# A transformer layer on one core: the product p @ w_ple computed beside the mixer's last blocks, not beside the last gate

## What is computed

```python
for i in range(DEPTH):                                  # DEPTH = 1
    proj = rms_norm(h, norm_mix[i]) @ w_in[i]           # q, k, v of two attention mixers A and B
    oa = sliding_window_sink_attention(...)             # 8 heads, window of 128
    ob = differential_attention(...)                    # 4 heads, 8 query blocks of 128 each
    h = h + jnp.concatenate([oa, ob], axis=-1) @ w_out[i]
    h = h + gated_conv_ffn(rms_norm(h, norm_ffn[i]), ...)
    gate = jax.nn.sigmoid(rms_norm(h, norm_ple[i]) @ w_ple_gate[i])
    h = h + gate * (p[i] @ w_ple[i])                    # p: 1024 x 256, w_ple: 256 x 1024
return rms_norm(h, norm_final)
```

## Time and profile before

| | before |
|---|---|
| median of 3 runs (range) | 1261.01 us (1259.12 to 1261.21) |
| the profiled execution, its own time | 1262.01 us |
| its span in the trace | 1259.9 us |
| TensorE busy | 1219.5 us (97%) |
| VectorE busy | 868.3 us (69%) |
| ScalarE busy | 517.3 us (41%) |
| mean granted TensorE clock | 0.99 |

### The profile page before, as it was taken

The page is one execution under the profiler, slowest core; times in us unless marked ns, Lnnn a source line. Parts: engine busy times, 40 slices in busy tenths (PEclk is TensorE's granted clock), DMA queues, the critical chain, the costliest instruction groups (busy, mean ns, idle before and its releaser), DMA issues.

```text
span 1259.9 us, 17110 instructions
## 1 busy us (share of the span) xinstructions
PE 1219.5 (97%) x6167; PEld 1004.0 (80%) x6167; DVE 868.3 (69%) x1510; ACT 517.3 (41%) x1042; POOL 248.5 (20%) x291
## 2 busy tenths in 40 slices
PE   8999999999789999999999999999999999999997
PEld 7997787887667787888888888888888888888885
DVE  5423786777886466887787777877677898964442
ACT  4311664665664224433333333333344444643321
POOL 0000000354454122232323323223120000000000
PEclk9999999999899999999999999999999999999998
DMA  7464233112833411333332323223398533620101
GB/s 210 91 89 87 51 85 84 31 43 72 219 124 61 141 50 59 101 110 99 112 98 85 125 88 122 84 84 125 135 326 317 174 94 104 222 67 25 43 34 50
DMA packets 128668, 136.07 MB, mean 108 GB/s; under 512 B 15570, under 2 KB 93130, under 8 KB 128522
## 3 DMA queue, kind: packets, MB, share of 16 engines
q1 hardware_dynamic: 128586, 135.00, 35.6%
HBM read 96.77 MB, written 37.22 MB: 106 GB/s over the span
## 4 chain that ended last, share of the span: by engine, by line
PE 63%; issue 2%; DVE 2%; DMA 1%; SPq 0%; ACT 0%; POOL 0%; POOLq 0%; DVEq 0%
PE ps L1687 62%; PE ps L1693 1%; DMA act_t<-mix_a 1%; DVE xs L1453 0%; PE ps L1927 0%; DVE h L1448 0%; DVE conv L1392 0%; SPq L479 0%; POOL stat L678 0%; ACT xs L787 0%; DVE act_t L1167 0%; PE ps L2077 0%; DVE gel L1680 0%; DVE h L1669 0%; DVE conv L1666 0%
## 5 line engine op out<-in xcount | busy, mean ns | idle before, releaser
L1687 PE MATMUL ps<-act_t,wbuf 128*128 128x512 f32 x1200 | 290.0, 398 | 2.9 <-DVE wbuf L1167 2.9
L1687 PEld LDWEIGHTS ps<-act_t,wbuf 128*128 128x128 f32 x1200 | 226.7, 189 | 57.8 <-issue 3.3
L1687 PE MATMUL ps<-wbuf 128*128 128x512 f32 x912 | 215.5, 391 | 0.0
L1687 PEld LDWEIGHTS ps<-wbuf 128*128 128x128 f32 x912 | 170.6, 188 | 36.2
L1687 PE MATMUL ps<-act_t,wq 128*128 128x512 f32 x624 | 155.7, 402 | 3.6 <-DVE wq L1169 2.8
L1687 PEld LDWEIGHTS ps<-act_t,wq 128*128 128x128 f32 x624 | 114.6, 188 | 33.5 <-issue 7.4
L678 POOL TENSOR_TENSOR stat<-stat 128x1 f32<-128x1 f32 x32 | 17.6, 549 | 437.9 <-DVE stat L1176 437.9
L784 ACT ACTIVATE wbuf<-raw 128x512 fp32r<-128x512 f32 (+1 forms) x107 | 69.0, 647 | 79.4 <-PE ps L1687 65.4
L1167 DVE TENSOR_TENSOR wbuf<-raw,wbuf 128x512 fp32r<-128x512 f32 (+1 forms) x107 | 87.6, 819 | 13.4 <-ACT wbuf L784 13.1
L1687 PE MATMUL ps<-hx,wbuf 128*128 128x512 f32 x408 | 96.2, 391 | 0.0
L1687 PEld LDWEIGHTS ps<-hx,wbuf 128*128 128x128 f32 x408 | 76.5, 188 | 16.6
(11 more groups left out here) (203 smaller groups left out, 2003.5 us busy)
## 6 DMA issues: line engine op xcount, KB each, us to landing
u_ops<-wbuf_f SPq DMA_DIRECT2D x77, 256.0 KB, 2.2
raw<-u_ops SPq DMA_DIRECT2D x77, 256.0 KB, 2.8
raw<-in_w_ffn_in SPq DMA_DIRECT2D x33, 512.0 KB, 3.9
g_ffn<-in_w_ffn_in SPq DMA_DIRECT2D x11, 512.0 KB, 4.1
act_f<-in_w_ffn_out SPq DMA_DIRECT2D x21, 256.0 KB, 3.7
w_raw<-in_w_in SPq DMA_DIRECT2D x10, 512.0 KB, 4.7
wbuf_f<-in_w_ffn_out SPq DMA_DIRECT2D x18, 256.0 KB, 6.7
x_in<-in_x SPq DMA_DIRECT2D x8, 512.0 KB, 3.8
```

The costliest lines, as they stand in the source:

```text
L1687: return nc.tensor.matmul(dst, lhs, rhs, start=start, stop=stop)
```

## The change

The product `p @ w_ple` (16 units of six matmuls, u = 0 to 15, one for half a token tile) goes from the gate to mixer B. Its steps:

- SP loads p and w_ple whole, 1 MB each, just after the third weight tile (`p_all`, `wp_all`). After units 3, 4, 5 and 6 TensorE turns two tiles of p (four transposes). ScalarE and VectorE make the high and low parts of two items each time (an item is two turned tiles of p, or a quarter of w_ple, 128x512), in a staging buffer of two places (`a_t`), and SP stores each to memory (`pw_ops`). Item i waits until item i-2 is stored. The wait ahead of mixer A's first scores is now for the last item. `load_w(4)` stands behind the first four stores and `load_w(5)` behind all eight.
- In mixer B the parts come back to `hx` and to row 4 of `act_t`. `p_unit` is the filler of blocks 21 to 31 and of n = 32 by the table `P_AT`: one each, but two in 25, 26, 27 and 32. The second of a block goes between the transposes and `b_pv`. ScalarE copies each result to one of four staging places (`p_stage`), between its exponentials and its square, and SP stores it (`pw_mem`). Block 28's scores wait for the copies of the units of 27.
- All 16 c_units move behind the last block: 2, 3, 3, 3 and 5 at n = 32 to 36 (`C_AT`), in the tile order 4 to 7, 0 to 3. `mix_c`, `mix_45` and most residual loads are sent in another order. The output projection has rows 4, 5, 6, 7 of tile 1, then of tile 0, and then rows 2 and 3 of both. `mix_a_back(3)` is sent from ScalarE's queue, beside `mix_a_back(2)` on SP's.
- In the gate stage the transposes of p, the 12 matmuls, the splits of p and w_ple and their PSUM banks are gone. The gate alternates between two pairs of banks; VectorE reads the product from a buffer that SP loads (`pw_buf`).

```diff
@@ SP, first projections
+        sp.dma_start(p_all, p.rearrange("(t q) n -> q t n", q=P)).then_inc(p_loaded[0], 16)
+        sp.dma_start(wp_all, w_ple.rearrange("(k q) n -> q k n", q=P)).then_inc(p_loaded[1], 16)
...
-        for j in range(3, 6):
-            load_w(j)
+        load_w(3)
+        for i in range(4):
+            item_store(i)
+        load_w(4)
+        for i in range(4, NITEM):
+            item_store(i)
+        load_w(5)
@@ ScalarE
+        def item_hi(i):
+            if i % 2 == 0:
+                act.wait_ge(S.tr0, NT + i // 2 + 1)
+            else:
+                act.wait_ge(p_loaded[1], 16)
+            if i >= 2:
+                act.wait_ge(pw_st[i % 2], 16 * (i // 2))
+            copy(item_dst(i, 0), item_src(i), S.xhi0)
...
+            for u in p_units(n):
+                act.wait_ge(S.p_unit, u + 1)
+                if u >= 4:
+                    act.wait_ge(p_st[u % 4], 16 * (u // 4))
+                copy(p_stage(u), ps[:, p_bank(u), :], S.p_out)
...
+        act.wait_ge(S.c_done, 2 * NT)
+        mix_a_back(act, 3, S.mix_23)
@@ the tables
-    C_FROM = 22
+    C_AT = (0, 2, 5, 8, 11, 16)
+    C_TILE = (4, 5, 6, 7, 0, 1, 2, 3)
+    P_AT = {21: 1, 22: 1, 23: 1, 24: 1, 25: 2, 26: 2, 27: 2, 28: 1, 29: 1, 30: 1, 31: 1, 32: 2}
-    O_ROWS = (4, 5, 6, 2, 3, 7)
+    O_ROWS = (4, 5, 6, 7, 2, 3)
@@ TensorE
         for u in range(FIRST_UNITS):
             unit(u)
-        pe.wait_ge(S.vlo, NT)
+            if 3 <= u < 7:
+                pe.wait_ge(p_loaded[0], 16)
+                pe.wait_ge(S.vlo, NT)
+                for e in range(2):
+                    for k in range(KP):
+                        at = DPLE * e + P * k
+                        ins = nc.tensor.transpose(item_bank(2 * u - 6)[:, at:at + P],
+                                                  p_all[:, 2 * (u - 3) + e, k * P:(k + 1) * P], ident[:, :])
+                ins.then_inc(S.tr0, 1)
+        pe.wait_ge(S.xlo0, NT + NITEM)
         pe.wait_ge(S.unit_lo, 6)
...
+            if n == 28:
+                pe.wait_ge(S.p_out, p_units(n)[0])
...
-            for k in range(KP):
-                for n, (a, b) in enumerate(SPLIT3):
-                    for half in range(2):
-                        ins = mm(ps[:, 5 + half, :], pt[:, t % 2, a, k * P:(k + 1) * P],
-                                 wp[:, b, k, HALF * half:HALF * (half + 1)],
-                                 k == 0 and n == 0, k == KP - 1 and n == 2)
-            ins.then_inc(S.pp_done, 1)
```

More of the change, by code:

```diff
@@ L259, in build, with items_stored, item_bank, item_src @@
     ut = wbuf[:, 10 * D:14 * D].rearrange("p (s l n) -> p s l n", s=2, l=2)
-    pt = wbuf[:, 14 * D:15 * D].rearrange("p (s l n) -> p s l n", s=2, l=2)
-    wp = wbuf[:, 6 * D:10 * D].rearrange("p (l k n) -> p l k n", l=2, k=KP)
     g_ple, g_fin = g_ffn, raw[:, 2, :]
-    p_in = xs[:, 1, :].rearrange("p (s n) -> p s n", s=2)
     u_ops = nc.dram_tensor("u_ops", (7, NQ, P, HALF), F32).ap()
     h_mem = nc.dram_tensor("h_mem", (NT, P, D), F32).ap()
-    names = """a_stored ident_ready cols_in cols_t onehot_in brow_t brow_ready brow_out bias_in consts_in
+    NITEM = 2 * NT // 2
+    NPU = 2 * NT
+    pw_ops = nc.dram_tensor("pw_ops", (NITEM, P, D), F32).ap()
+    pw_mem = nc.dram_tensor("pw_mem", (NT, P, D), F32).ap()
+    p_all = e_t[:, 0].rearrange("p m (t n) -> p (m t) n", n=DPLE)
+    wp_all = e_t[:, 1]
+    def items_stored(eng):
+        for e in range(2):
+            eng.wait_ge(pw_st[e], 16 * (NITEM // 2))
+    def item_bank(i):
+        return ps[:, 2 + i // 2, :]
+    def item_src(i):
+        return item_bank(i) if i % 2 == 0 else wp_all[:, i // 4, HALF * (i // 2 % 2):HALF * (i // 2 % 2 + 1)]
+    def item_dst(i, part):
+        return a_t[:, i % 2, HALF * part:HALF * (part + 1)]
+    P_AT = {21: 1, 22: 1, 23: 1, 24: 1, 25: 2, 26: 2, 27: 2, 28: 1, 29: 1, 30: 1, 31: 1, 32: 2}
+    def p_units(n):
+        first = sum(c for b, c in P_AT.items() if b < n)
+        return range(first, first + P_AT.get(n, 0))
+    def p_bank(u):
+        at = [p_units(n).index(u) for n in P_AT if u in p_units(n)][0]
+        return 2 * at
+    def pt(t, part, k):
+        at = HALF * part + DPLE * (t % 2) + P * k
+        return act_t[:, t // 2 % 2, 4, at:at + P]
+    def wp(part, k, half):
+        return hx[:, 2 * part + k, HALF * half:HALF * (half + 1)]
+    def gate_bank(t):
+        return ps[:, 3:5, :] if t % 2 else ps[:, 5:7, :]
+    def p_stage(u):
+        at = (KD * (u % 4 // 2) + 5) * SEQ + HALF * (u % 2)
+        return act_f[:, at:at + HALF]
+    names = """a_stored ident_ready rows_in cols_t brow_t brow_ready brow_out bias_in consts_in
     consts_ready consts_scaled gain_in sq0 ms0 pow0 xs0_ready tr0 xhi0 xlo0 wv_hi wv_lo vproj vhi vlo vshift
@@ L648, in _, with load_pw @@
         sp.wait_ge(S.op_lo, NPROD + 2 * (6 * NQ + 8))
-        for k in range(KP):
[L650 to L657, removed]
+        def load_pw(t):
+            sp.dma_start(pw_buf(t), pw_mem[t]).then_inc(p_loaded[t % 2], 16)
+        load_pw(0)
+        load_pw(1)
+        for t in range(NT):
+            if t + 2 < NT:
+                sp.wait_ge(S.gated, t + 1)
+                load_pw(t + 2)
             sp.wait_ge(S.o_ready, t + 1)
@@ L1247, in _ @@
                 split_w((u + 3) // 2)
+            if 3 <= u < 7:
+                for i in (2 * u - 6, 2 * u - 5):
+                    dve.wait_ge(S.xhi0, NT + i + 1)
+                    low(item_dst(i, 1), item_src(i), item_dst(i, 0), S.xlo0)
         next_w = [5]
@@ L1762, in c_unit @@
         def c_unit(c):
-            t, half = c // 2, c % 2
+            t, half = C_TILE[c // 2], c % 2
             if c == 0:
@@ L1866, in _ @@
                 unit(FIRST_UNITS + b_fill(n) // 2, b_fill(n) % 2)
+            for u in p_units(n)[:1]:
+                p_unit(u)
+            if n == NBS:
+                for u in p_units(n)[1:]:
+                    pe.wait_ge(S.b_exp, 2 * NBS)
+                    p_unit(u)
             for c in c_units(n):
@@ L1879, in _ @@
                 ins.then_inc(S.b_turned, 1)
+            if n < NBS:
+                for u in p_units(n)[1:]:
+                    p_unit(u)
             if 2 <= n <= NBS + 1:
@@ L1906, in oproj @@
                 ins.then_inc(S.oproj, 1)
[L1908 to L1911 removed]
+        for n in (2, 3, 4):
+            for c in c_units(NBS + n):
+                c_unit(c)
+            if n < 4:
+                y_turn(NBS + n)
         oproj(1, O_ROWS[:2])
[L1913 removed]
+        pe.wait_ge(S.b_ylo, 3 * NT)
+        oproj(1, O_ROWS[2:3])
+        pe.wait_ge(S.b_ylo, NBS)
+        oproj(1, O_ROWS[3:4])
         pe.wait_ge(S.c_added, 2 * NT)
[L1915 to L1923 removed]
+        oproj(0, O_ROWS[:4])
+        oproj(0, O_ROWS[4:])
+        oproj(1, O_ROWS[4:])
         def turn4(src, bank):
```

201 lines of the change are left out of this document (103 added, 98 removed).

## The result

| | before | changed |
|---|---|---|
| median, with the runs of this comparison | 1260.47 us (1259.12 to 1261.21) | 1270.14 us (1266.53 to 1270.53) |
| ratio, 95% interval | | 1.0064 [1.0039, 1.0088] |
| the same, run again in 5 rounds | 1262.16 us | 1269.57 us; 1.0066 [1.0048, 1.0083] |
| the profiled execution, its span | 1259.9 us | 1264.4 us |

The change makes the kernel slower by 0.65%, about 8 us. I had forecast 1263.0 us, in a range to 1268.5, and the measured 1270.14 lies beyond it. The sum had forecast 2.0 us more than before, where the ratio gives 8.1: the sign was right, but 6 us were missing.

What follows compares the result with a forecast made beforehand. TensorE was taken as full in mixer A, the FFN and the gate, with gaps only in mixer B and its end. -23.0 + 8.3 + 4.4 + 12.3 = +2.0 on 1261.0 gave 1263.0 us, eight in ten from 1256.0 to 1268.5.

Steps and rivals of the forecast that it cites:

- 1. Gate: Gate stage: 96 matmuls and 16 transposes leave, less 1.1 us for an exposed sigmoid: -23.0 us, bounds -23.2 and -22.8.
- 2. First units: Before mixer A: transposes 1.75 us, wait for the last item 5.0, half clock 1.5: +8.3 us, bounds 4.5 and 11.
- weight tile 3 late: Rival, before mixer A: tile 3 lands 4.5 us later, wait 7.5 us; +2.5 on the forecast, 1265.5 us, chance 0.17.
- 3. Blocks 21 to 31: Mixer B: four more units than before and ScalarE's copies lengthen blocks: +4.4 us, bounds 2.5 and 7.
- 4. Mixer's end: After the last block: 180 matmuls instead of 108, wait for mixer A's rows 0.4 us: +12.3 us, bounds 10.5 and 14.5.
- my fourth rival: Mixer's end: gains and h tiles share the queues, rows come 2 us late, clock drops: +3.7, 1266.7 us, chance 0.06.
- the cheap hand-over: Rival, before mixer A: stores land in time, clock stays up, blocks' gaps absorb half the new units: 1257.3 us, chance 0.30.

Runs made afterwards that it cites:

- the run with the loads alone: Kernel before, with only the two 1 MB loads of p and w_ple added ahead of weight tile 3, read by nothing: 1260.52 us, ratio 0.9999.
- the run with one issuer: The kernel with both edits, but all eight transfers of mixer A's rows 2 and 3 sent from SP: 1255.44 us, run again 1255.81 us.
- the kernel with both edits: Changed kernel with the items one unit earlier and the FFN's gains and weight loads held until rows 2 and 3 landed: 1256.90 us, ratio 0.9966.
- the run with all copies on VectorE: The kernel with both edits and one issuer, with VectorE instead of ScalarE copying the results of p by w_ple: 1256.73 us, ratio 0.9965.
- the one with the loads held: Changed kernel, with SP sending the FFN's gains and first three weight tiles only after rows 2 and 3 landed: 1266.02 us, ratio 1.0029.

## Why the prediction was wrong, step by step

The sum was +2.0 us on the profiled execution. The ratio of five rounds says +8.3. Two steps failed: the wait ahead of mixer A was sized too small, and the transfer that TensorE waits for at the mixer's end was priced by its bytes and without the loads that follow it.

- **1. Gate, -23.0.** Measured -22.7, 0.1 outside its bounds. The mechanism was right, with the exposed sigmoid.
- **2. First units, +8.3.** Failed in size, not in kind. The chain was the one that I wrote down, in its order, and tile 4 was sent at 114.34, where my chain put it at 105.6 + 8.9 = 114.5. What I had too small: its landing, 4.1 us by the earlier trace rows, was 5.3 from issue to split; tile 3's delay, 2.0, was 2.5; and from the split of tile 4 to mixer A it took 8.4 us, not 7.7. The wait was 7.31 and 6.74 us, not 5.0. The clock cost 1.5, as I had it. The step measured +10.6 (9.1 and 1.5). The rival "weight tile 3 late" had the right size for another reason, and the run with the loads alone excludes it. I also took the place of the items as given. The same chain, one unit earlier, costs nothing but the transposes; that run shows that the units had the room.
- **3. Blocks 21 to 31, +4.4.** Measured +4.5, but from other members. From one block's scores to the next one's, changed less before, for blocks 21 to 30: 0.75, -0.91, 0.61, 0.11, 1.42, 0.36, 0.88, -0.38, 0.19, 0.15; and from block 31's scores to the filler of n = 32: 1.32. Block 25 is as forecast (1.4), 27 is half (0.9 for 1.6), and for 31 I had 0.2. TensorE needs the bank of block 31's unit again at once, and ScalarE's copy of it stands behind the exponentials; I had charged such a wait to the first c_unit only. Moving that one copy took 1.2 of it away.
- **4. Mixer's end, +12.3.** The step that failed most: it measured +17.2, outside its bounds of 10.5 to 14.5. Work and small waits were about right. (In the second profile of the changed kernel this stretch is 59.95 us, 2.3 more than in the first.) "I take 1.5 + 9.4 = 10.9 us, against a cover of 48 matmuls" was wrong twice. Alone, the rows take 12.3 to 13.3 us with one issuer or two (eight runs, 12.7 in the mean), not 10.9: their bytes at 228 GB/s were no measure of them (they move in pieces of 512 bytes; whether that is the cause was not tried), and the earlier trace rows had shown 12.0, with 13.5 in the other profile of the same code. I had explained that row by the issuing time, which the run with one issuer refutes. And the gains and the FFN's loads share the queues, another 2 to 3 us (14.6 to 15.95 in four runs). So the wait was 3.4 and 4.8, not 0.4, and the clock took 1.4 to 2.3 us after it (from the end of the wait to the first transposes 11.27 and 12.21 us, 9.88 at full clock). This is the mechanism of my fourth rival, to which I gave 0.06; I looked for the sharers among the gains and h tiles, and not for what SP sends next once its wait for the split of w_out is met sooner.
- **The base.** The profiled execution of before had a start that was 3 us late, which is in only one other profile (82.05); against a usual one its own distance to mine would have been larger. This hid 2.8 us in the comparison of the two profiles, not in the ratio.

Sum of what was missed, in us: 2.3 in step 2, 0.1 in 3, 4.9 in 4, 0.3 in 1, together 7.6, so 9.6 with the 2.0 of the sum; 1.0 and 2.3 came back between the mixer and the gate in the two profiles, which leaves the 8.3 of the ratio within 1 us. Why that stretch varies by 2 us from run to run was not tried. A second pair of profiles, the changed kernel again against the two loads alone, gives +8.5 for the first units, +6.1 for mixer A and the blocks, +17.5 for the mixer's end, +0.3 up to the gate and -22.5 for the gate; with 0.2 at the start that is the 10.1 between their spans. So the four steps measure the same in both pairs within 0.6 us, only the stretch up to the gate does not (-2.3 and +0.3), and the 8.3 of the ratio lies between the two sums (7.3 without the late start, and 10.1).

Of the rivals, the cheap hand-over (1257.3) comes close to the 1256.9 of the kernel with both edits, but that is luck. Its parts were 4.5, 2.5 and 12.3 us; that run, against the profile of before, measured 1.7 for the first units (no wait at all, not one of 2.7), 3.8 for mixer A and the blocks, and 14.1 for the mixer's end.

## What to carry to other kernels

When a step is moved, list what its queue sends next and what that now overtakes: here a weight tile sent sooner let three FFN loads run against the transfer that TensorE waited for, and a weight load put behind four stores made a chain of 22 us. If a chain of copy, store and load must end by a fixed point, move its start before shortening its links: one unit earlier was worth 8.8 us and cost a changed index. Price a transfer by the duration of the same transfer in the trace, not by its bytes and the best rate, and a second issuer at nothing until a run shows otherwise.

## What the runs showed of the hardware

- Eight transfers of 2 MB in all took 12.3 to 12.8 us with one issuer (four runs, issuing 6.6 to 7.4 us) and 12.5 to 13.3 with two (four runs), with nothing sent behind them. With the gains and three FFN tiles, 512 KB each, sent behind them they took 14.6 to 15.95 (four runs); with a w_out tile and the gains behind them, in the order of the kernel before, 12.1 and 13.5. All these run from the first issue to TensorE's restart.
- The granted clock after waits of TensorE at the mixer's end: after 1.35 us, and after 1.72 in the run with both edits, it stayed at 1.00 (2.4 GHz); after 1.90 us (the run with all copies on VectorE, at n = 32) and after 2.16 us it was 0.50 (1.2 GHz) in the next window. In the wait of 7.31 us it fell before the wait was over: 0.81 in 122 to 124, 0.50 from 124 on.

The run with one issuer, then the one with the loads held, windows of 2 us as above:

```profile
434.00:436.00 2.00, 2.00 (x10) 1.64 (x9) 0.00 (x0) 0.00 (x0) 0.00 (x0) 1.00 0.89 248
```

```profile
442.00:444.00 2.00, 2.00 (x6) 1.61 (x5) 0.00 (x0) 0.00 (x0) 0.00 (x0) 0.50 0.92 235
```

Ten matmuls in one window, six in the other: here a wait that is 0.8 us longer costs its length and 1.5 us more (from its end to the first transposes 11.43 us against 9.88).
